# Retention's two chunks of heads moved into common stages, with one chunk's factor in the second dilated queries' tile and the other's behind it

## The reference

```python
def retention_mixer(cols, norm_w, pos):
    B, S, _ = cols.shape
    q, k, v, g = jnp.split(cols, 4, axis=-1)
    shp = (B, S, RET_HEADS, HEAD_DIM)
    o = retention_chunkwise(rotary(q.reshape(shp), pos), rotary(k.reshape(shp), pos),
                            v.reshape(shp).astype(jnp.float32))
    mu = jnp.mean(o, axis=-1, keepdims=True)
    var = jnp.mean(jnp.square(o - mu), axis=-1, keepdims=True)
    o = (o - mu) * lax.rsqrt(var + NORM_EPS) * norm_w.astype(jnp.float32)
    o = o.reshape(B, S, RET_W)
    return (jax.nn.silu(g.astype(jnp.float32)) * o).astype(cols.dtype)
```

## Time and profile before

| | us |
|---|---|
| median of 3 runs | 1221.32 (1220.82 to 1221.42) |
| the profiled execution | 1222.44 |
| its span | 1221.10 |
| PE busy in it | 1186.7 |
| DVE busy | 811.0 |
| ACT busy | 697.3 |
| POOL busy | 279.2 |

### The profile page before, as it was taken

How to read it: one execution, slowest core, us unless ns; L and a number is a source line. 1 busy time by engine, 2 the same in 40 slices (tenths; PEclk the granted TensorE clock), 3 DMA queues, 4 the chain that set the end, 5 groups by cost and what they waited for, 6 DMA issues and landing times.

```text
span 1221.1 us, 18869 instructions
## 1 busy us (share of the span) xinstructions
PE 1186.7 (97%) x7688; PEld 1059.2 (87%) x7688; DVE 811.0 (66%) x1044; ACT 697.3 (57%) x962; POOL 279.2 (23%) x181
## 2 busy tenths in 40 slices
PE   9998899999999999999999899999999989999997
PEld 9888899999998888888999688888899977888886
DVE  7877978777566866676878455555556973555454
ACT  6698666685535443435646856445554397555543
POOL 0000000001401111111475522122225654222211
PEclk9999999999999999999999999999999999999999
DMA  9644655544546655554643346655464533565560
GB/s 283 199 147 141 208 192 180 180 138 164 204 161 234 210 199 176 201 176 139 193 138 121 104 139 209 204 195 181 161 189 141 170 106 108 174 228 187 182 207 34
DMA packets 152437, 210.66 MB, mean 173 GB/s; under 512 B 5504, under 2 KB 132640, under 8 KB 151712
## 3 DMA queue, kind: packets, MB, share of 16 engines
q1 hardware_dynamic: 151584, 205.08, 52.0%
q10 hardware_dynamic: 768, 4.39, 1.0%
HBM read 208.37 MB, written 1.08 MB: 172 GB/s over the span
## 4 chain that ended last, share of the span: by engine, by line
PE 75%; DVE 11%; ACT 10%; issue 3%; DMA 1%; POOL 0%; SPq 0%; ACTq 0%; DVEq 0%
PE banks L537 73%; ACT w_hi L1014 3%; DVE w_lo L1404 2%; ACT tmp L1014 2%; DVE xbc L1412 2%; ACT L1014 2%; PE banks L545 1%; ACT probs_dil L1014 1%; DMA raw<-in_w_in 1%; DVE tmp L1412 1%; DVE work L1408 1%; DVE lru_u L1412 1%; DVE tmp L1404 1%; ACT lru_ab L1014 1%; ACT probs_dsa L1014 0%
## 5 line engine op out<-in xcount | busy, mean ns | idle before, releaser
L537 PE MATMUL banks<-act,w_hi 128*128 128x256 f32 (+1 forms) x2928 | 681.5, 321 | 6.0 <-ACT w_hi L1014 2.6
L537 PEld LDWEIGHTS banks<-act,w_hi 128*128 128x128 f32 x2928 | 481.2, 191 | 53.9 <-issue 9.5
L537 PE MATMUL banks<-act,w_lo 128*128 128x256 f32 x1896 | 521.8, 282 | 0.0
L1404 DVE TENSOR_TENSOR w_lo<-raw,w_hi 128x2048 fp32r<-128x2048 f32 (+4 forms) x174 | 375.9, 2162 | 206.9 <-ACT w_hi L1014 206.2
L1014 ACT ACTIVATE w_hi<-raw 128x2048 fp32r<-128x2048 f32 (+1 forms) x191 | 359.6, 1884 | 187.2 <-PE banks L537 185.0
L537 PEld LDWEIGHTS banks<-act,w_lo 128*128 128x128 f32 x1896 | 355.4, 191 | 1.4
L537 PE MATMUL banks<-w_hi,act 128*128 128x512 f32 (+1 forms) x1072 | 323.1, 376 | 7.1 <-DVE act L1404 6.5
L537 PEld LDWEIGHTS banks<-w_hi,act 128*128 128x128 f32 x1072 | 197.3, 190 | 46.8 <-issue 11.0
L2002 POOL TENSOR_TENSOR act<-tmp,act 128x512 fp32r<-128x512 f32 x44 | 102.5, 2329 | 439.6 <-ACT act L1014 439.6
L2002 POOL TENSOR_TENSOR w_lo<-raw,w_hi 128x512 fp32r<-128x512 f32 (+1 forms) x120 | 156.3, 1333 | 203.9 <-ACT w_hi L1014 203.9
L537 PE MATMUL banks<-w_lo,act 128*128 128x512 f32 (+1 forms) x536 | 200.1, 373 | 0.0
(11 more groups left out here) (236 smaller groups left out, 828.7 us busy)
## 6 DMA issues: line engine op xcount, KB each, us to landing
raw<-in_w_in SPq DMA_DIRECT2D x64, 1024.0 KB, 5.3
raw<-in_w_up SPq DMA_DIRECT2D x32, 1024.0 KB, 5.4
raw<-in_w_down SPq DMA_DIRECT2D x32, 1024.0 KB, 5.1
raw<-in_w_ffn_in SPq DMA_DIRECT2D x22, 1024.0 KB, 5.1
raw<-in_w_out SPq DMA_DIRECT2D x12, 1024.0 KB, 5.0
raw<-in_w_ffn_out SPq DMA_DIRECT2D x11, 1024.0 KB, 4.9
raw<-in_w_out_ssm SPq DMA_DIRECT2D x8, 1024.0 KB, 4.9
raw<-in_w_out_lru SPq DMA_DIRECT2D x5, 1024.0 KB, 4.8
```

The lines of the kernel that those rows point to most:

```text
L537: return mm_ops.matmul(out, lhs, rhs, start=start, stop=stop, skip_group_check=True)
L1404: return ops.tensor_tensor(out, a, b, op)
```

## The change

The stages are placed anew, in both layers. Both chunks do step 0 in `dil_k` 0, step 1 in `dil_q` 0, step 2 in `dil_v` 0 and step 3 in `dil_k` 1. Step 4, now DVE's factor alone, comes in the middle of `dil_q` 1 for chunk 0 and behind that tile for chunk 1. ACT's high part becomes step 5 and DVE's low part step 6. Both lie in the middle of `dil_v` 1, the high parts first, and the low parts after the dilated attention's step 3.

As both chunks are now in step 0 at once, `decayed` gets two more buffers, which are parts of `tmp` 0 and 1, and its guard asks for the chunk before the last. The banks of steps 2 and 3 all come from the ring `high`.

```diff
-        put("mid", ("dil_k", 2 * l), ("ret", l, 0, 0))
+        put("mid", ("dil_k", 2 * l), ("ret", l, 0, 0), ("ret", l, 1, 0))
         put("after", ("dil_k", 2 * l), ("sel_top", l, 2))
-        put("mid", ("dil_q", 2 * l), ("ret", l, 0, 1), ("ret", l, 1, 0))
+        put("mid", ("dil_q", 2 * l), ("ret", l, 0, 1), ("ret", l, 1, 1))
         put("after", ("dil_q", 2 * l), ("sel_top", l, 3), ("sel_need", l))
-        put("mid", ("dil_v", 2 * l), ("ret", l, 0, 2), ("ret", l, 1, 1), ("att", l, "dil0", 0))
+        put("mid", ("dil_v", 2 * l), ("ret", l, 0, 2), ("ret", l, 1, 2), ("att", l, "dil0", 0))
         put("after", ("dil_v", 2 * l), ("sel_keep", l))
-        put("mid", ("dil_k", 2 * l + 1), ("ret", l, 0, 3), ("ret", l, 1, 2), ("att", l, "dil0", 1), ("att", l, "dsa", 0))
-        put("mid", ("dil_q", 2 * l + 1), ("ret", l, 0, 4), ("att", l, "dil0", 2), ("ret", l, 1, 3))
-        put("mid", ("dil_v", 2 * l + 1), ("ret", l, 1, 4), ("ret", l, 0, 5), ("att", l, "dil0", 3),
-            ("ret", l, 1, 5), ("att", l, "dsa", 1), ("att", l, "dil1", 0))
+        put("mid", ("dil_k", 2 * l + 1), ("ret", l, 0, 3), ("ret", l, 1, 3), ("att", l, "dil0", 1), ("att", l, "dsa", 0))
+        put("mid", ("dil_q", 2 * l + 1), ("ret", l, 0, 4), ("att", l, "dil0", 2))
+        put("after", ("dil_q", 2 * l + 1), ("ret", l, 1, 4))
+        put("mid", ("dil_v", 2 * l + 1), ("ret", l, 0, 5), ("ret", l, 1, 5), ("att", l, "dil0", 3), ("ret", l, 0, 6), ("ret", l, 1, 6),
+            ("att", l, "dsa", 1), ("att", l, "dil1", 0))
@@
-        decayed = [sb(f"decayed_{i}", [P, KQ], stack=two) for i in range(2)]
+        decayed = [sb(f"decayed_{i}", [P, KQ], stack=two) for i in range(2)] + [tmp[0][:, 0:KQ], tmp[1][:, 0:KQ]]
@@ PE
-                    bank = take(high if ch else low, ("ret_mean", n), at("ro_c", n + 1))
+                    bank = take(high, ("ret_mean", n), at("ro_c", n + 1))
-                    bank = take(low if ch else high, ("ret_var", n), at("ret_root", n + 1))
+                    bank = take(high, ("ret_var", n), at("ret_root", n + 1))
@@ ACT
-                if step == 4:
+                if step == 5:
                     act.wait_ge(*at("ret_x", n + 1))
@@ DVE
-                        bank, m, dec = psum["ret_s", s], decayed[h % 2], c["decay"][:, h * SEQ:(h + 1) * SEQ]
+                        bank, m, dec = psum["ret_s", s], decayed[h], c["decay"][:, h * SEQ:(h + 1) * SEQ]
                         vec.wait_ge(*at("ret_s", s + 1))
-                        vec.wait_ge(*at("ret_o", n))
+                        vec.wait_ge(*at("ret_o", n - 1))
-                if step == 5:
+                if step == 6:
                     vec.wait_ge(*at("ret_hi", n + 1))
```

More of the change, by code:

```diff
@@ L918, in ret @@
                     for h in (2 * ch, 2 * ch + 1):
-                        inst = value_product(bank[(h % 2) * HD:(h % 2 + 1) * HD, 0:SEQ], decayed[h % 2],
+                        inst = value_product(bank[(h % 2) * HD:(h % 2 + 1) * HD, 0:SEQ], decayed[h],
                                              rv[:, 0, h * HD:(h + 1) * HD], rv[:, 1, h * HD:(h + 1) * HD])
```

## The result

The changed kernel takes 1214.61 us (1213.73 to 1216.0), the kernel before 1221.37 (1220.82 to 1223.14) in the same comparison: a ratio of 0.9943, interval 0.9926 to 0.9960, or 6.8 us less. The profiled execution took 1213.86 us with a span of 1212.6.

What follows compares the result with a forecast made beforehand. PE, busy 97% of the span, was taken to bound the kernel. Per layer -1.9 us at both waits and +1.45 for the clock make -0.45, -0.9 in two layers, from 1221.32 to 1220.4; range 1217.2 to 1222.0.

Steps and rivals of the forecast that it cites:

- ACT's chain from the scaling at 678.87: ACT's unbroken work from the `probs_dsa` scaling until PE's bank is freed at 686.49, taken as unchanged at 7.62 us.
- Both roots together: Joining both chunks' square roots on ACT cuts table loads from 4 to 2 per layer; `w_hi` moves from 672.11 to 671.0.
- The half clock: PE's half clock moves to blocks 2 and 3 of `out_2` 0, behind the 3.0 us wait, costing 1.45 us per layer.
- The inference on the clock: After PE's second wait of 3.0 us the clock surely falls, since it fell after 3.0 and 1.9 us before.
- rival 2: The clock stays up in `out_2` 0; gain 1.9 us per layer, -3.8 in all, 1217.5; chance 0.14.
- ACT's `w_hi`: ACT's `w_hi`, at 672.11 in the kernel before, starts at 671.0.
- retention's low parts end: DVE's two retention subtractions, queued between POOL's pieces, end at 675.5 and 676.9; the last ended at 678.76 before.
- PE's second wait: PE's wait inside `out_2` 0 for ACT's `probs_t`, from 681.6 to 684.6, 3.0 us; 1.5 in the kernel before.
- Rival 1: DVE gets in ahead of POOL at 674.1; scaling at 676.0, -1.45 us per layer, -2.9 in all, 1218.4; chance 0.22.
- Rivals 3 and 4: POOL taking further turns, 1223.2 or 1226.0, chance 0.08; and the loads going with 0 gained, 1221.3, chance 0.06.
- rival 3: `score` comparisons or a product lose one or two more POOL periods; +1.9 us, 1223.2, or +4.7, 1226.0; chance 0.08.
- The 0 for PE's regrouped products: Chunk 1's score products one tile earlier, value product following, cost PE 0: no matmul added or dropped.

Runs made afterwards that it cites:

- e1: Changed kernel plus a 1-column square root on ACT before the `probs_dsa` scaling, which puts the exponential's load back behind it; 1219.43 us, ratio 0.9975.
- e0: The changed kernel measured once more, beside its variants, against the kernel before; 1214.33 us, ratio 0.9936.
- e4: Changed kernel with retention's two low parts in one DVE subtraction of 512 columns instead of two of 256; 1212.52 us, ratio 0.9921.
- e7: Changed kernel with chunk 1's factor at the end of the middle of `dil_q` 1 instead of behind that tile; 1214.95 us, ratio 0.9941.
- e3: Changed kernel with only chunk 1's step 3, its root, put back in the middle of `dil_q` 1; 1225.36 us, ratio 1.0025.
- e8: As e3, with chunk 1's variance product taking its bank from the ring `low` again, as in the kernel before; 1222.69 us, ratio 0.9999.

## Why the prediction was wrong

**The step that failed** is the sentence on ACT's chain from the scaling at 678.87: "That is 7.62 us, and it stays." Further on, under *Both roots together*, the prediction itself says that of four table loads two remain. The fourth of them, the exponential's at 680.38, is inside these 7.62 us and is one of the two that go. I took the loads off in one place, ahead of the `w_hi`, and carried the chain's length over whole. It is 6.22 us now. e1 puts just this load back and costs 1.4 us per layer without a fall of the clock.

**The half clock hung on this error.** With 1.3 us too much in the chain I had PE wait 3.0 us and charged 1.45 for the clock. The wait is 1.65 and the clock does not fall, in neither layer of the profiles of after, e0, e4 and e7, whose second waits are all 1.65 to 1.69. Rightly put together, my own rows give 1.9 + 1.3 = 3.2 us per layer, 1214.9 in all; 3.5 per layer and 1214.6 were measured.

**The inference on the clock was too sure as well.** The prediction took falls after 3.0 and 1.9 us of idle PE and wrote "3.0 is well on the falling side". e1 shows one fall and one not after 3.07 and 3.05 us, e3 the same after 3.06 and 3.09, and the run after shows none after the 1.83 us that brought one before. Had the wait been 3.0, the clock would have cost its 1.6 us only part of the time. The sign of rival 2 (clock at 1.00 throughout) came, but not its time: it held 1217.5, because it too kept the 7.62. It did name "the chance that the wait comes out near the 1.5 us that did no harm"; it had no reason why the wait should, and the lost load is that reason.

**What held.** In the times of the kernel before, that is plus the 1.81 us by which `lq_t` starts earlier (668.33 less 666.52):

| | forecast | measured |
|---|---|---|
| ACT's `w_hi` | 671.0 | 670.9 |
| retention's low parts end | 676.9 | 676.9 |
| scaling of `probs_dsa` | 677.0 | 677.0 |
| PE's first wait | 1.1 | 1.16 |
| blocks 0 and 1 of `out_2` 0 | 2.84 | 2.85 |
| PE's second wait | 3.0 | 1.65 |

Rival 1 did not come: POOL was ahead. Rivals 3 and 4 did not either, but e8's layer 1 shows rival 3's mechanism, one more turn of POOL for a small shift. The 0 for PE's regrouped products was 0.2: the `dil1` scores in `dil_v` 1 start 1.81 us earlier than in the run before (670.10 for 671.91), the `ret` scores in `dil_k` 0 only 1.60 (631.55 for 633.15), with no wait between them in either. This, and the 0.1 by which the chain lost more than the load's 1.29, is what 3.5 has over 3.2.

## What to carry to other kernels

When an operation that forces a table load moves, two loads move: its own and the one that brings the old table back. Find both on the chain of waits, and build each chain anew from its rows; a length measured on the old kernel must be searched for what the change removes before it is reused. Join the functions of one table. Join small operations of DVE with two SBUF operands that run beside POOL, since there each can cost a turn: two of 256 columns took 2.87 us and one of 512 took 1.73.

## What the runs showed of the hardware

- Whether the granted clock falls after an idle stretch of PE isn't settled by the length of this stretch alone: the same 1.8 us of idle PE before 40 brought 0.50 in seven of the eleven profiles and 1.00 in four, and 3.05 us was followed by 1.00 and 3.07 us by 0.50 in one execution. What else decides was not tried. The Trainium skill, "TensorE: Matmul & The Clock Gate", section "What's actually happening", says that the hardware counts time freely and not from the kernel's start, by which such a place may fall out differently from one execution to the next; that the profiles differ at this place agrees with it.
- A subtraction of 512 columns beside POOL took 1.73 us, two of 256 took 2.87. In the Trainium skill, "SBUF — State Buffer", section "SBUF: two separate sides", such operations of DVE and POOL hold one port pair in turn, each for a whole instruction; the 1.14 us between them, near the 1.38 us that one of POOL's pieces takes beside them in the mean, agree with it.
